# Staging the token-side operands of a down projection through the sync engine's queue

## The reference

```
def _sq_relu_mlp(h, w_up, w_down):
    a = jax.nn.relu(h @ w_up)
    return (a * a) @ w_down

# w_up is 1024 x 4096, w_down 4096 x 1024
x = x + _sq_relu_mlp(_rmsnorm(x, g_mlp), w_up, w_down)
return _rmsnorm(x, g_final)
```

## Time and profile before

| | |
|---|---|
| time, median of 3 runs | 1693.84 us (1692.42 to 1695.14) |
| the profiled execution, whole | 1690.91 us |
| its span, first to last instruction | 1689.0 us |
| mean granted TensorE clock | 0.992 |
| TensorE busy | 1625.0 us, 96% |
| VectorE / ScalarE / GpSimd busy | 882.3 / 643.0 / 121.8 us |
| stores to `op_rows`, GpSimd's queue | 224 of 256 KB, 58.73 MB |
| transfers on SyncE's queue | 145.47 MB |

### The profile page before, as it was taken

How to read it: one execution, slowest core, us unless ns; L and a number is a source line. 1 busy time by engine, 2 the same in 40 slices (tenths; PEclk the granted TensorE clock), 3 DMA queues, 4 the chain that set the end, 5 groups by cost and what they waited for, 6 DMA issues and landing times.

```text
span 1689.0 us, 23114 instructions
## 1 busy us (share of the span) xinstructions
PE 1625.0 (96%) x8400; PEld 1380.2 (82%) x8400; DVE 882.3 (52%) x1543; ACT 643.0 (38%) x1074; POOL 121.8 (7%) x228
## 2 busy tenths in 40 slices
PE   5899999999999799999999999999999999999996
PEld 4788888888888688898888887888888878888885
DVE  6544444444444443663254165555555567676767
ACT  5445545455554552341044043333333331212222
POOL 0000000000000000000000002333333320000000
PEclk9999999999999999999999999999999999999998
DMA  5011010010100133042111012666666798676752
GB/s 191 16 27 27 14 53 15 26 40 24 29 27 26 58 107 98 26 149 75 50 38 50 26 50 98 216 221 213 213 213 212 251 381 308 223 274 224 273 187 114
DMA packets 151312, 205.34 MB, mean 122 GB/s; under 512 B 8209, under 2 KB 91281, under 8 KB 151217
## 3 DMA queue, kind: packets, MB, share of 16 engines
q1 hardware_dynamic: 133312, 145.47, 26.1%
q0 software_dynamic: 17920, 58.73, 9.9%
HBM read 141.13 MB, written 63.57 MB: 121 GB/s over the span
## 4 chain that ended last, share of the span: by engine, by line
PE 87%; DVE 5%; ACT 4%; DMA 2%; issue 2%; SPq 0%; DVEq 0%
PE psG L650 15%; PE psG L633 12%; PE psG L635 12%; PE psG L634 12%; PE psS L991 8%; PE psO L782 7%; PE psO L991 4%; PE psG L991 4%; PE psS L731 4%; PE psG L713 3%; PE psS L662 2%; PE psS L661 2%; PE psS L917 1%; DMA act_hi<-op_rows 1%; PE psS L678 1%
## 5 line engine op out<-in xcount | busy, mean ns | idle before, releaser
L633 PE MATMUL psG<-act_hi,w_hi 128*128 128x512 f32 x640 | 249.6, 390 | 2.4 <-DVE act_lo L1291 2.4
L635 PE MATMUL psG<-act_hi,w_lo 128*128 128x512 f32 x640 | 249.0, 389 | 0.0
L634 PE MATMUL psG<-act_lo,w_hi 128*128 128x512 f32 x640 | 249.0, 389 | 0.0
L782 PEld LDWEIGHTS psO<-V,pT 128*128 128x128 f32 x1152 | 148.4, 193 | 18.9 <-ACT pT L1097 6.9
L650 PE MATMUL psG<-act_hi,w_hi 128*128 128x512 f32 x368 | 152.7, 415 | 3.5 <-DVE act_lo L1291 3.5
L1097 ACT ACTIVATE pT<-psS 128x1024 f32<-128x1024 f32 (+7 forms) x128 | 83.6, 653 | 187.4 <-PE psS L731 184.7
L650 PE MATMUL psG<-act_hi,w_lo 128*128 128x512 f32 x368 | 154.7, 420 | 0.0
L625 POOL DMA_DIRECT2D op_rows<-a_hi x112 | 60.8, 543 | 1247.1 <-DVE a_lo L1291 1239.1
L782 PE MATMUL psO<-V,pT 128*128 128x64 f32 x1152 | 145.1, 272 | 5.2 <-ACT pT L1097 5.2
L650 PE MATMUL psG<-act_lo,w_hi 128*128 128x512 f32 x368 | 149.5, 406 | 0.0
L633 PEld LDWEIGHTS psG<-act_hi,w_hi 128*128 128x128 f32 x640 | 120.1, 188 | 27.8 <-DVE act_lo L1291 2.6
(11 more groups left out here) (195 smaller groups left out, 3093.3 us busy)
## 6 DMA issues: line engine op xcount, KB each, us to landing
act_hi<-op_rows SPq DMA_DIRECT2D x38, 1024.0 KB, 7.3
op_rows<-a_hi POOLq DMA_DIRECT2D x112, 256.0 KB, 2.8
op_rows<-a_lo POOLq DMA_DIRECT2D x112, 256.0 KB, 3.4
act_lo<-op_rows SPq DMA_DIRECT2D x18, 1024.0 KB, 7.4
raw<-in_w_up_dram SPq DMA_DIRECT2D x32, 512.0 KB, 4.7
raw<-in_w_in_dram SPq DMA_DIRECT2D x22, 512.0 KB, 3.9
qB<-in_w_down_dram SPq DMA_DIRECT2D x8, 1024.0 KB, 9.6
act_late<-in_w_down_dram SPq DMA_DIRECT2D x8, 1024.0 KB, 11.8
```

The costliest lines, as they stand in the source:

```text
L633: nc.tensor.matmul(dst, sh, mh, start=(k == 0), stop=False)
L634: nc.tensor.matmul(dst, sh, ml, start=False, stop=False)
L635: mm = nc.tensor.matmul(dst, sl, mh, start=False, stop=(k == n - 1))
L782: mm = nc.tensor.matmul(psO[:, u % 2, 0:HEAD], pT[:, b * P:(b + 1) * P], V[par][:, b, h * HEAD:(h + 1) * HEAD], start=(b == 0), stop=(b == ...
```

## The change

GpSimd's loop is gone. SyncE stores each operand with one transfer of 512 KB: the high and low part now form one tile `a_op[i]` (128 x 2 x 512), at the addresses that the two had before, and in `op_rows` the two parts of a partition stand side by side (4 KB in a run, where they were two runs of 2 KB in two places). Loads back still take one part each, 2 KB in a run. Each store raises `op_stored[i]` by 16 in place of twice 16. The stores stand in SyncE's list between the loads of weights, each behind a wait for its own low part.

```
--- before.py
+++ after.py
@@ -163,7 +163,7 @@
 
     w_in_k, w_out_k, w_xq_k, w_xk_k, w_xv_k, w_xo_k, w_up_k = map(
         k_rows, (w_in, w_out, w_xq, w_xk, w_xv, w_xo, w_up))
-    op_rows = nc.dram_tensor("op_rows", (D_FF // 256, 7, 2, P, HALF), f32).ap()
+    op_rows = nc.dram_tensor("op_rows", (D_FF // 256, 7, P, 2, HALF), f32).ap()
     bias_rows = nc.dram_tensor("bias_rows", (2 * PAIRS, 8, T), f32).ap()
 
     base = 16 * KB + 448
@@ -240,8 +240,9 @@
 
     a_sq = [at(f"a_sq{j}", [P, HALF], f32, 98 + 2 * j) for j in range(4)]
     a_sum = [at(f"a_sum{j}", [P, HALF], f32, 150 + 2 * j) for j in range(4)]
-    a_hi = [at(f"a_hi{i}", [P, HALF], f32r, 158 + 4 * i) for i in range(7)]
-    a_lo = [at(f"a_lo{i}", [P, HALF], f32r, 160 + 4 * i) for i in range(7)]
+    a_op = [at(f"a_op{i}", [P, 2, HALF], f32r, 158 + 4 * i) for i in range(7)]
+    a_hi = [a_op[i][:, 0, :] for i in range(7)]
+    a_lo = [a_op[i][:, 1, :] for i in range(7)]
 
     early, late = slice(0, HALF), slice(HALF, T)
 
@@ -561,17 +562,39 @@
                 if m == 5:
                     sp.wait_ge(tile_done, G_XO)
                     gain(3, x_gain, g_mlp)
-            with sp.Fori(0, DOWN_GROUPS) as g:
+            def op_store(q, i):
+                sp.wait_ge(a_lo_done, q * 7 + (i + 1))
+                dst = op_rows[bass.ds(q, 1), i, :, :, :].rearrange("o p a n -> (o p) a n")
+                sp.dma_start(dst, a_op[i][:].bitcast(f32)).then_inc(op_stored[i], 16)
+
+            def up_block(q, g, kk, i):
+                raw_block(q * 2 + (C_MLP + i), i, w_up_k[:, :, bass.ds(g * T + (i * HALF + kk * P), P)], cols)
+
+            def up_loads(q, g, kk):
+                up_block(q, g, kk, 0)
+                op_store(q - 2, 0)
+                up_block(q, g, kk, 1)
+                for i in range(1, 7):
+                    op_store(q - 2, i)
+
+            for q in range(4):
+                if q < 2:
+                    up_block(q, 0, q, 0)
+                    up_block(q, 0, q, 1)
+                else:
+                    up_loads(q, 0, q)
+            with sp.Fori(1, DOWN_GROUPS) as g:
                 for kk in range(4):
-                    for i in range(2):
-                        raw_block(g * 8 + (C_MLP + 2 * kk + i), i, w_up_k[:, :, bass.ds(g * T + (i * HALF + kk * P), P)], cols)
+                    up_loads(g * 4 + kk, g, kk)
+            for i in range(7):
+                op_store(QUADS - 2, i)
 
             def op_load(n):
                 g, pos = divmod(n, 7)
                 i = OPS.index(DOWN[pos][0])
-                sp.wait_ge(op_stored[i], 32 * 4 * (g + 1))
+                sp.wait_ge(op_stored[i], 16 * 4 * (g + 1))
                 for part in range(2):
-                    src = op_rows[4 * g:4 * g + 4, i, part, :, :].rearrange("k p n -> p k n")
+                    src = op_rows[4 * g:4 * g + 4, i, :, part, :].rearrange("k p n -> p k n")
                     sp.dma_start(opA[n % 3][part].bitcast(f32), src).then_inc(op_loaded[n % 3], 16)
 
             def w_quarter(name, dst, g, ff, half):
@@ -583,12 +606,16 @@
             gain(4, f_gain, g_final)
             sp.wait_ge(lo_done, B_BLOCKS + C_MLP + 2 * QUADS)
             w_quarter("B21", B21, 0, 1, 0)
+            op_store(QUADS - 1, 0)
+            op_store(QUADS - 1, 1)
             sp.wait_ge(tile_done, G_MLP + 4 * QUADS - 2)
             op_load(0)
             op_load(1)
             sp.wait_ge(tile_done, G_MLP + 4 * QUADS)
             w_quarter("B12", B12, 0, 0, 1)
             w_quarter("B22", B22, 0, 1, 1)
+            for i in range(2, 7):
+                op_store(QUADS - 1, i)
             op_load(2)
             for n in range(N_PARTS - 3):
                 g, pos = divmod(n, 7)
@@ -615,14 +642,6 @@
                 sp.wait_ge(out_stored[i], 16 * TT // 2)
 
 
-        @block.gpsimd
-        def _(pool):
-            with pool.Fori(0, QUADS) as q:
-                for i in range(7):
-                    pool.wait_ge(a_lo_done, q * 7 + (i + 1))
-                    for part, src in enumerate((a_hi[i], a_lo[i])):
-                        dst = op_rows[bass.ds(q, 1), i, part, :, :].rearrange("o p n -> (o p) n")
-                        pool.dma_start(dst, src[:].bitcast(f32)).then_inc(op_stored[i], 16)
 
         @block.tensor
         def _(pe):
@@ -1237,9 +1256,9 @@
             def a_hi_out(q, name, first):
                 i = OPS.index(name)
                 if not first:
-                    act.wait_ge(op_stored[i], q * 32)
+                    act.wait_ge(op_stored[i], q * 16)
                 act.wait_ge(a_made, q * 8 + MADE[name])
-                nc.scalar.activation(a_hi[i][:], a_tile(name)[:], ACT.Copy).then_inc(a_hi_done, 1)
+                nc.scalar.activation(a_hi[i], a_tile(name)[:], ACT.Copy).then_inc(a_hi_done, 1)
 
             def up_quad(q, par, first=False, last=False):
                 for j in range(4):
@@ -1652,7 +1671,7 @@
             def up_lo(q, name):
                 i = OPS.index(name)
                 dve.wait_ge(a_hi_done, q * 7 + (i + 1))
-                lo_part(a_lo[i][:], a_tile(name)[:], a_hi[i][:], a_lo_done)
+                lo_part(a_lo[i], a_tile(name)[:], a_hi[i], a_lo_done)
 
             def up_sum(q, name, a, b, op):
                 dve.wait_ge(a_made, q * 8 + (MADE[name] - 1))
```

## The result

The changed kernel takes 1704.92 us (median of 6 runs, 1701.53 to 1705.79), the kernel before 1694.49 us (1692.42 to 1695.87, 6 runs). The ratio is 1.0059, with a 95% interval of 1.0048 to 1.0069: slower by 10 us. The forecast was 1700.4 us in a range of 1696.3 to 1706.0, slower.

A forecast was written before the change was run, and what follows sets the result against it. TensorE's matmuls, end to end but for two holes between the stages, 2.9 us together, were taken as the bound. 0 (up stage) + 6.6 (part 2) on 1693.84 us gave 1700.4 us, range 1696.3 to 1706.0.

The forecast's parts named there:

- rival B: Change of stages: transfers bind longer, full rings hold SyncE's issues back; +9.5 to +13, about 1705 us; chance 0.18.
- Stores in the up stage: Up stage loop: stores moved to SyncE cost nothing, hidden by a quad of slack; 0 us, bounds 0 and 1.
- B11's issue: End of up stage: behind quad 14's seven stores, B11 is issued near 1351.3 us, where it was 1321.98.
- Load 0's issue: Ahead of part 0: behind A12's store, load 0's halves go at 1365.7 and 1366.1 us, where it was 1355.07.
- Load 0's transfer: Ahead of part 0: load 0 lands at 1373.3 us, so part 0 starts 6.3 us later, bounds +4.2 and +13.6.
- The clock: Start of part 0: after 7.5 us idle TensorE runs at half speed; costs 2.0 us, bounds 0 and 2.7.
- Rival A: Part 0: same late load, but the clock stays up or returns at once; +4.6, 1698.4 us; chance 0.17.
- Part 2: Down stage: TensorE's work sets its start at 1397.2 us, load 2 landing at 1395.1; delay 6.6 us.
- C: Change of stages: gaps of SyncE and the DMA engines absorb the delay; +1 to +3, about 1695.5 us; chance 0.08.
- D: Change of stages: SyncE's single stores raise the rate, both holes (2.9 us) close; 1690.9 us; chance 0.02.
- E: Up stage: a load of weights in the loop stalls it, costing over 15 us; chance 0.03.

The follow-up runs named there:

- layout-only: Kernel before with one tile and one 512 KB store per operand, still issued by GpSimd; 1693.09 us, ratio 0.9996 to the kernel before.
- reordered: Changed kernel with B11 and gain ahead of quad 14's stores, and loads 0, 1 and 2 ahead of the last quad's stores; 1690.46 us.
- kept-warm: Changed kernel with 85 identity transposes on TensorE between the up stage and part 0; 1702.33 us, ratio 1.0047 to the kernel before.
- B11 early: Changed kernel with B11 and the gain issued ahead of the seven stores of quad 14; 1699.02 us, ratio 1.0027 to the kernel before.
- loads first: Changed kernel with loads 0 and 1 ahead of the last quad's store of A12, B11 still late; 1698.78 us.
- all loads first: Changed kernel with loads 0, 1 and 2 ahead of the last quad's stores, B11 and gain still behind quad 14's stores; 1696.66 us.
- load 2 first: Kernel before, GpSimd's stores kept, with load 2 moved ahead of B12 and B22 in SyncE's list; 1699.40 us.
- two moves: Changed kernel with B11 early and loads 0, 1 ahead of the last quad's A11 and A12 stores, five stores still ahead of load 2; 1696.11 us.
- waits-only: Kernel before, GpSimd's stores kept, with three waits for low parts added to SyncE's list, ahead of B11, load 0 and load 2; 1701.67 us.

## Why the prediction was right, and what was too small

The direction, the place and the causes in the chain were as forecast; the size was 6.6 us, and 10.0 were measured (10.3 at this place in the profile). The 3.6 us between are 1.3 us at B11's issue, 1.5 us in load 0's transfer and 0.8 us of the clock. That the time still lies in the range is owed to the part of the range that was drawn for rival B. Times here are from the start of the up stage's last matmul.

- **Stores in the up stage, 0 us: right.** TensorE gained no wait in that stage, and the layout-only kernel measures the store's form at 0.
- **B11's issue: mis-sized.** Forecast at -14.2 us, measured at -12.95. I had priced five stores at the pace of VectorE's low parts, 2.9 us to the end of the last. SyncE needed 4.12 us. The first four went out 0.6 us apart, at that pace; but the fourth issue took 1.07 us and the fifth 1.20, where the first took 0.33. B11's transfer then took 7.7 us, as forecast (7.8).
- **Load 0's issue**: forecast at +0.2, measured at +1.5. This is B11's 1.3 us carried on; the steps of ScalarE and VectorE between them were right.
- **Load 0's transfer: mis-sized.** I took 7.6 us from the first issue to landing, after the pair at 1477 of the earlier trace rows; it was 9.1 us. With B11's share, part 0 starts at +10.6 in place of +7.8, and these 2.8 us are the larger part of the error.
- **The clock: right in kind, too small.** I took 2.0 us with 2.7 as the upper bound. Parts 0 and 1 took 24.7 us against the 21.9 forecast at full clock, 2.8 us more. The rows from 1379.62 to about 1385.6 at half level make 3.0 us. The size varies: in the four other kernels with a hole of 4 us or more ahead of part 0, parts 0 and 1 took 1.5 to 2.6 us longer than 21.9 us, waits taken off, so 2.0 us lies among them and the changed kernel's profile above them all. Rival A, that the clock stays up, is out: it fell in the changed kernel and in six kernels with a hole of 3.3 us or more that nothing filled (all but the reordered, layout-only and kept-warm ones). By the rule cited from the Trainium skill, "TensorE: Matmul & The Clock Gate", the drop was certain, and the trace agrees.
- **Part 2: right in kind.** TensorE's own work decided its start, there was no hole ahead of it, and the old 1.7 us went. Both paths came later than forecast: TensorE's at +35.28 for +31.7, and load 2 at +33.8 for +29.6. Load 2 was through 1.5 us ahead of TensorE, where the forecast had 2.1.

Rival B (the transfers bind longer) had the size, +9.5 to +13, and the sense of its conditions, but neither of their numbers: load 0 landed at +10.6, which is 1376.1 in the times of the kernel before (B: 1377 to 1380), and load 2 at +33.8, or 1399.3 (B: 1400 to 1404). Its slow issues did show, in the last two stores ahead of B11, with far less than 8 MB outstanding; SyncE's long gap ahead of load 0 is a wait for A12's low part. The truth lay between the forecast and B. C, D and E didn't occur. D's argument, that load 0 can't go while a wait stands ahead of it, is what the reordered kernel turned round: with the waits behind the loads, both holes of the kernel before close, and the stores on SyncE's queue cost nothing that is seen.

Moving B11 alone brought part 2 forward by 4.5 us, where 2.4 to 3.4 were expected: 3.4 us are load 0's earlier issue, 0.7 us a shorter transfer of it (8.4 us in place of 9.1, from first issue to part 0), and 0.4 us less from part 0 to part 2, in which a new wait of 0.4 us for load 2 is counted. Why the same pair of transfers takes 7.9 us (at 1477 in the kernel before), 8.4 or 9.1 us out of a queue that seems empty was not settled; no kernel was made for it.

## What to carry to other kernels

A queue of transfers is a list in program order: before a transfer is moved onto an engine that issues loads, look at what each of its waits now stands ahead of, above all where one stage ends and the next must be fed. A transfer whose data nobody needs soon belongs behind every load that is due, and the order among loads follows when the engines' own work on them has to start. An idle stretch on TensorE is priced with the microseconds at half clock that follow it: at this change of stages, every hole of 3.3 us or more was followed by them, and none of up to 2.0 us was.

## What was not expected of the hardware

**A hole of the same length lowers the clock in one execution and not in another.** At the start of the up stage TensorE is idle for 2.37 or 2.38 us in the profile of every one of the eleven kernels. The stretches of the changed kernel there (columns as in the earlier trace rows):

```profile
1028.00:1030.00 2.00, 0.00 (x0) 0.00 (x0) 1.39 (x2) 1.43 (x2) 0.00 (x0) 1.00 0.00 0
1030.00:1032.00 2.00, 1.77 (x5) 1.44 (x6) 0.77 (x2) 0.00 (x0) 0.00 (x0) 0.64 0.20 80
1032.00:1034.00 2.00, 2.00 (x7) 1.52 (x6) 0.00 (x0) 0.00 (x0) 0.00 (x0) 0.51 0.93 250
```

And of the kernel before, 2 us earlier in its span:

```profile
1026.00:1028.00 2.00, 0.00 (x0) 0.00 (x0) 1.39 (x2) 1.54 (x2) 0.00 (x0) 1.00 0.00 0
1028.00:1030.00 2.00, 1.66 (x7) 1.40 (x8) 0.89 (x2) 0.00 (x0) 0.35 (x1) 1.00 0.00 0
1030.00:1032.00 2.00, 2.00 (x10) 1.65 (x10) 0.00 (x0) 0.00 (x0) 0.87 (x2) 1.00 0.50 182
```

The work is the same, and the clock was at the half level for some 3.5 us in one and 1.00 in the other. In the profiles of the other kernels the clock dipped at this place in those with B11 early, loads first, layout only, all loads first, load 2 first and two moves, and not in the reordered, waits-only and kept-warm ones. This accounts for 1.6 of the 3.5 us by which the changed kernel's profile is late before its last up matmul. The other 1.9 us are there when the up stage starts. Ahead of it the clock was lower in the changed kernel's profile from 200 to 225 us (0.93 against 1.00) and from 550 to 600 us (0.86 against 0.90), which is where they may come from; they were not followed further. The medians, which differ by 10.4 us, agree with the 10.3 us at the change of stages, so these dips are not the change's. Places within a profile have to be compared from a common event, not from the span's start.

**Issue time on SyncE depends on what is in flight.** A quarter of `w_down` is issued in 0.38 us into a quiet queue and in 1.20 us behind five stores of 512 KB (1356.09 above). It seems to be SyncE's own queue that counts: in the waits-only kernel GpSimd's stores are under way at the same point (DMA share 0.93 from 1352 to 1354), and B11, the gain and B21 are issued in 0.38, 0.55 and 0.46 us. That is one comparison and not an experiment made for it.
